# Scores, units and output projection of the first mixer in one loop: a two-layer, two-block transformer in fp32 on one core

## What is computed

```
xn = rms_norm(x, attn_norm); h = xn @ w_in          # 1024 x 2848
cq, ckv, kr, dq, dk, dv, gq, gk, gv = split(h)      # 384 256 32 512 512 512 384 128 128
q_a = rms_norm(cq) @ w_uq; k_a, v_a = rms_norm(ckv) @ w_ukv   # latent (MLA), 6 heads of 96
o_a = attention(rope(norm(q_a)), rope(norm([k_a, kr])), v_a)  # 6 maps
o_b = att(dq1, dk1, dv) - lambda * att(dq2, dk2, dv)          # differential, 4 heads, 8 maps
o_b = rms_norm(o_b) * out_gain * (1 - lambda_init)
o_c = attention(rope(norm(gq)), rope(norm(gk)), gv)           # grouped, 6 heads on 2
x = x + concat(o_a, o_b, o_c) @ w_o                 # 1280 x 1024
x = x + ffn(rms_norm(x))
```

## Time and profile before

| | |
|---|---|
| median of three runs | 2550.3 us (2546.77 to 2550.85) |
| the profiled execution | 2550.99 us, its span 2549.1 us, mean granted clock 0.944 |
| PE busy | 2344.8 us, 92% of the span |
| DVE busy | 1809.2 us, 71% |
| ACT busy | 1435.6 us, 56% |
| DMA | 570.81 MB, mean 224 GB/s |

### The profile page before, as it was taken

The page is one execution under the profiler, slowest core; times in us unless marked ns, Lnnn a source line. Parts: engine busy times, 40 slices in busy tenths (PEclk is TensorE's granted clock), DMA queues, the critical chain, the costliest instruction groups (busy, mean ns, idle before and its releaser), DMA issues. The chain is left out here.

```text
span 2549.1 us, 30005 instructions
## 1 busy us (share of the span) xinstructions
PE 2344.8 (92%) x11100; PEld 1959.6 (77%) x11100; DVE 1809.2 (71%) x2496; ACT 1435.6 (56%) x2065; POOL 76.6 (3%) x71
## 2 busy tenths in 40 slices
PE   6788999968899899889989969999999999999997
PEld 5677787757688678768877868888888888888885
DVE  4955455784555556555555657989898989898988
ACT  4433444442444444444444537878787878787876
POOL 0100000110000100000010000000000000000000
PEclk9867999986899999999999979999999999999999
DMA  6402555420455553445554337999999999999996
GB/s 238 138 1 83 190 189 183 155 93 1 143 182 188 172 181 116 133 162 186 190 185 133 113 110 262 375 334 378 337 375 339 376 338 372 341 370 338 369 347 243
DMA packets 157175, 570.81 MB, mean 224 GB/s; under 512 B 18496, under 2 KB 18816, under 8 KB 156384
## 3 DMA queue, kind: packets, MB, share of 16 engines
q1 hardware_dynamic: 153424, 553.48, 62.1%
q0 software_dynamic: 3600, 15.35, 1.8%
HBM read 567.71 MB, written 1.05 MB: 223 GB/s over the span
## 5 line engine op out<-in xcount | busy, mean ns | idle before, releaser
L368 DVE TENSOR_TENSOR w_lo<-raw,w_hi 128x1024 fp32r<-128x1024 f32 x1051 | 1270.0, 1224 | 439.7 <-ACT w_hi L362 412.0
L362 ACT CAST w_hi<-raw 128x1024 fp32r<-128x1024 f32 x1051 | 1099.0, 1052 | 472.5 <-PE bank L416 451.8
L414 PE MATMUL bank<-w_hi,x_hi 128*128 128x512 f32 (+1 forms) x2864 | 1135.0, 396 | 44.1 <-DVE x_lo L454 23.7
L416 PE MATMUL bank<-w_hi,x_lo 128*128 128x512 f32 (+1 forms) x2864 | 1114.7, 389 | 0.0
L415 PE MATMUL bank<-w_lo,x_hi 128*128 128x512 f32 (+1 forms) x2864 | 1113.0, 389 | 0.0
L414 PEld LDWEIGHTS bank<-w_hi,x_hi 128*128 128x128 f32 x2864 | 544.0, 190 | 153.8 <-issue 25.1
L416 PEld LDWEIGHTS bank<-w_hi,x_lo 128*128 128x128 f32 x2864 | 542.6, 189 | 112.9
L415 PEld LDWEIGHTS bank<-w_lo,x_hi 128*128 128x128 f32 x2864 | 544.7, 190 | 103.8
L747 PE MATMUL bank<-arena,PT 128*128 128x64 f32 (+1 forms) x576 | 96.2, 326 | 2.2 <-DVE O L764 2.2
L705 ACT ACTIVATE PP<-bank,small 128x256 f32<-128x256 f32 x80 | 37.1, 469 | 107.9 <-DVE small L695 107.9
L747 PEld LDWEIGHTS bank<-arena,PT 128*128 128x128 f32 x576 | 93.7, 247 | 2.6 <-DVE PT L734 2.4
(11 more groups left out here) (181 smaller groups left out, 1365.4 us busy)
## 6 DMA issues: line engine op xcount, KB each, us to landing
raw<-in_stream SPq DMA_DIRECT2D x1051, 512.0 KB, 5.6
tab<-in_lngb POOLq DMA_DIRECT2D x5, 1024.0 KB, 5.2
arena<-in_rpb POOLq DMA_DIRECT2D x16, 256.0 KB, 5.1
arena<-in_bgate POOLq DMA_DIRECT2D x4, 512.0 KB, 5.0
tab<-in_rowv POOLq DMA_DIRECT2D x2, 640.0 KB, 8.3
X<-in_x SPq DMA_DIRECT2D x1, 1024.0 KB, 5.2
out_y<-X SPq DMA_DIRECT2D x2, 512.0 KB, 2.8
tab<-in_ropec POOLq DMA_DIRECT2D x2, 448.0 KB, 5.1
```

Of the source, the lines that this page charges most:

```text
L362: nc.scalar.copy(w_hi[:, s % SPLIT, :], raw[:, slot, :]).then_inc(hi_done, 1)
L368: e.tensor_tensor(w_lo[:, s % SPLIT, :], raw[:, s % RAW, :], w_hi[:, s % SPLIT, :].bitcast(F32), ALU.subtract).then_inc(lo_done, 1)
L414: pe.matmul(out, xh, wh, start=first, stop=False)
L416: return pe.matmul(out, xl, wh, start=False, stop=last)
```

## The change

Four things; they act in `first_layer`, and `attention` and `unit` serve the second mixer too:

1. `w_in` is cut at the borders of its parts, seven chunks instead of six (two more halves per layer, the same columns), and the stream is reordered: cq, ckv+kr, dq, dk, then `w_uq`, `w_ukv`, then dv, gq, gk+gv; the rows of `w_o` come in the order 3, 4, 5, 6, 0, 1, 2, 7, 8, 9. The units of cq and ckv stand inside chunk dq, the units of dk inside chunk dv.
2. `attention` takes `lag`: map m's exponentials are transposed `lag` steps after its scores. The first mixer uses 2, the second 1. The transposed maps always go to bank 2, the results to bank 3. ACT copies map m-lag before it takes the exponentials of map m. In the first mixer ACT makes all copies.
3. The loop of the first mixer now holds (`fill`) the six halves of gq and gk+gv in steps 0 to 10, the DVE work of the latent and grouped heads and the norm of the differential outputs, and eight of the ten halves of `w_o` in steps 15 to 22; and (`units`) the units of the latent heads in steps 6 to 11, of the grouped heads in 12 and 13, and of the outputs in 13, 15, 17, 19, 21. The maps come in the order differential, latent, grouped. Two halves of `w_o` follow the loop.
4. `unit` replaces `qk_stage`: one ACT and one DVE instruction for both blocks. The output gain of the differential heads is applied by the unit (`og_col`) instead of by DVE.

```diff
 def chunks_in1():
-    return [(c, min(512, W_IN1 - c)) for c in range(0, W_IN1, 512)]
+    return [(C_CQ, MQR), (C_CKV, MKVR + MROPE), (C_DQ, 2 * DH * DQ), (C_DK, 2 * DH * DQ), (C_DV, DH * DV),
+            (C_GQ, GH * GD), (C_GK, 2 * GKV * GD)]
...
+        def unit(E, bk, dst, srcs, w=P, scale=1.0, gains=None, lag=1):
...
+            if E.kind == "pe":
+
+                wait(e, qk_lo, E.qk.at(1 - lag))
+                for b, src in enumerate(srcs):
+                    for tb in range(TB):
+                        i = e.transpose(pb[:, b * S + tb * P:b * S + (tb + 1) * P], src(tb), ident[:, :])
+                i.then_inc(qk_full, 1)
...
-            for step in range(M + 2):
+            for step in range(M + lag + 1):
+                m = step - lag
+                if 0 <= m < M and E.kind == "act" and by_act(m):
+
+                    copy(m)
...
-                m = step - 1
+                m = step - lag
                 if 0 <= m < M:
                     g = E.map.at(m)
-                    tbk = bank[2 if packed else 2 + m % 2]
+                    tbk = bank[2]
                     if E.kind == "pe":
                         e.wait_ge(p_ready, g + 1)
 
-                        if packed:
-                            if m:
-                                e.wait_ge(*copied(m - 1))
-                        else:
-                            wait(e, (pt_act, pt_dve)[m % 2], g // 2)
+                        if m:
+                            e.wait_ge(*copied(m - 1))
+                        wait(e, qk_lo, E.b2)
...
-                m = step - 2
+                m = step - lag - 1
...
-                        wait(e, o_done, g + 1 - (1 if packed else 3))
+                        wait(e, o_done, g)
...
-                if aside:
-                    aside(step)
+                aside(step)
+                if units:
+                    if E.kind == "pe" and lag <= step < M + lag and units(step, True):
+
+                        e.wait_ge(*copied(step - lag))
+                    units(step)
...
+            def out_half(n):
...
+                if E.kind == "pe":
+                    e.wait_ge(qk_lo, E.qk.at())
...
+                E.half_step(use)
...
+            def fill(step):
+                if step in (0, 2, 4, 6, 7):
+                    next(gq, None)
+                if step in (8, 10, 11):
+                    if step == 8 and E.kind == "pe":
+                        e.wait_ge(qk_lo, E.qk.at())
+                    next(gkv, None)
+                if step >= 15:
+                    out_half(step - 15)
+                if step < 6:
+                    latent_heads(step)
+                    made["mla"] = E.qks.at()
+                if step in (7, 8, 9):
+                    grouped(step - 7, C_GQ, GH, F_GQ, at_g)
+                    made["gq"] = E.qks.at()
+                if step == 11:
+                    diff_norm(0)
+                    grouped(0, C_GK, GKV, F_GK, at_g + TB * GH)
+                if step == 12:
+                    diff_norm(1)
+                    made["diff"] = E.qks.at()
+                    grouped(1, C_GK, GKV, F_GK, at_g + TB * GH)
+                    grouped(2, C_GK, GKV, F_GK, at_g + TB * GH)
+                    made["gk"] = E.qks.at()
...
-            attention(E, maps, latent_heads)
...
-            tp_stage(E, O, MIX // P, 0)
-            gemm_rows(E, MIX // P, 0)
+            attention(E, maps, fill, act_copies=True, units=units, lag=2)
+            out_unit(2, 9, 1, 0)
+            for n in (8, 9):
+                out_half(n)
...
-            norm_transposes(E, colg[:, l, CG_FFN:CG_FFN + KD], 4)
+            norm_transposes(E, colg[:, l, CG_FFN:CG_FFN + KD], (2, 3))
...
-            attention(E, maps, lambda step: next(job, None), packed=True)
+            attention(E, maps, lambda step: next(job, None))
```

More of the change, by code:

```diff
@@ L118, in stream_order @@
     order = list(range(TOTAL))
+    late = sum(halves_of(w) for _, w in chunks_in1()[4:])
+    for l in range(LAYERS):
+        a = l * H_L1 + H_IN1 - late
+        b = l * H_L1 + H_IN1 + H_UQ + H_UKV
+        n = H_UQ + H_UKV
+        order[a:b] = list(range(b - n, b)) + list(range(a, b - n))
+        order[b:b + H_O] = [b + k for k in O_ORDER]
     for x in range(1, NE):
@@ L603, in turned, with pair_of @@
             return i
-        def lo_block(blk):
-            return qk_l[:, blk, :]
-        def qk_stage(E, units, scaled=(), alone=False):
+        def pair_of(blk, n=2, w=P):
+            return qk_t[0:w, blk:blk + n, :], qk_l[0:w, blk:blk + n, :]
+        def unit(E, bk, dst, srcs, w=P, scale=1.0, gains=None, lag=1):
             e = E.e
[L613 to L637, removed]
@@ L639, in attention @@
-        def attention(E, maps, aside=None, packed=False):
+            hi, lo = dst
+            nb = len(srcs)
+            pb = bank[bk][0:w, 0:nb * S]
+            p3 = pb.rearrange("p (b n) -> p b n", n=S)
+            if E.kind == "pe":
[4 more added lines that the diff above has]
+                i.then_inc(qk_full, 1)
@@ L642, in attention, with by_act, copy @@
+            E.qk.n += 1
+            if bk == 2:
+                E.b2 = E.qk.at()
+        def attention(E, maps, aside, act_copies=False, units=None, lag=1):
             e = E.e
             M = len(maps)
+            O_BANK = bank[3]
+            def by_act(m):
+                return act_copies or m % 2 == 0
             def copied(m):
+                n = sum(by_act(j) == by_act(m) for j in range(m + 1))
+                return (pt_act, E.pa.at(n)) if by_act(m) else (pt_dve, E.pd.at(n))
+            def copy(m):
@@ L724, in attention @@
                         i.then_inc(pt_full, 1)
[L726 to L734, removed]
-                m = step - 2
+                    if E.kind == "dve" and not by_act(m):
+                        copy(m)
+                m = step - lag - 1
                 if 0 <= m < M:
@@ L765, in attention @@
                         i.then_inc(o_done, 1)
-                if aside:
-                    aside(step)
+                aside(step)
[3 more added lines that the diff above has]
+                    units(step)
+            E.pa.n += sum(by_act(m) for m in range(M))
+            E.pd.n += sum(not by_act(m) for m in range(M))
             E.map.n += M
@@ L819, in first_layer, with columns, four @@
             at_l = at_g + TB * ng
-            def columns(c, w):
-                return H[:, :, c:c + w]
-            def beside(chunk, hx):
-                if hx == 0 and E.kind == "dve" and chunk > 1:
+            nq, nk = MQR // P, MKVR // P
+            gg = GH // GKV
+            b_gq, b_cq = 2 * nd // 2, 2 * nd // 2 + gg + 1
+            def columns(c, n):
+                return H[:, :, c:c + n]
+            def four(c, h, d):
+                return columns(c, h * d).rearrange("p t (h d) -> p t h d", h=h)
@@ new lines, in out_half, with use @@
+            def out_half(n):
+                def use(wh, wl):
+                    k = O_ORDER[n]
+                    for tb in range(TB):
+                        t = slice(tb * P, (tb + 1) * P)
+                        for c in range(2):
+                            w = slice(c * 512, (c + 1) * 512)
+                            i = mm3(e, bank[4 + 2 * tb + c][:, :], x_hi[:, k, t], x_lo[:, k, t], wh[:, w], wl[:, w],
+                                    n == 0, n == H_O - 1)
+                    return i
+                if E.kind == "pe":
+                    e.wait_ge(qk_lo, E.qk.at())
+                    if n == 0:
+                        e.wait_ge(acc_act, E.acc.at())
+                        e.wait_ge(acc_dve, E.acc.at())
+                E.half_step(use)
```

394 lines of the change are left out of this document (266 added, 128 removed).

## The result

The changed kernel takes **2505.5 us** (median of 4 runs, 2504.5 to 2506.8) against 2550.6 for the kernel before beside it; the ratio is 0.9827, 95% interval 0.981 to 0.9844. The prediction was 2506, in a range of 2470 to 2540. Disturbed executions at a far lower clock are left out of all medians (of the run with overlapped units one in six, at 3465.9 us, which was the profiled one).

The account below looks back on a forecast made before the run. PE, 92% busy, was taken to bound the kernel through its own time and idle stretches. Mixers -45.8, norm +2.4 and second mixer -0.8 sum to -44.2 on 2550.99, giving 2506 us, range 2470 to 2540.

Parts of the forecast that it names:

- Scores of layer 0 at 95: Before the first mixer's loop: the first scores begin at 95 us instead of 117.9, 23 us earlier.
- Steps 0 to 5, 27.6: Start of the first mixer's loop: DVE sets the pace; its work and its waits for ACT take 27.6 us.
- rival (a): Better overlap: DVE's waits for ACT vanish and the clock costs 2 instead of 10 us per layer; 2475 us, chance 0.20.
- Steps 6 to 14, 45.2: Middle of the first mixer's loop: DVE sets the pace; its work and waits take 45.2 us.
- the clock's 10: First mixer's loop: low PE clock adds 10 us per layer, between 2 (always full) and 25 (low from step 6 to 17).
- Rival (c): First mixer's loop, steps 0 to 14: engines take turns without overlap, 41.5 us more per layer; 2589 us, chance 0.07.
- Steps 15 to the residual, 48.0: End of the first mixer's loop and after: PE sets the pace, 48.0 us up to the residual of `w_o`.
- Clock, low around steps 9 to 15: First mixer's loop: as a sign of being right, clock near 0.5 only around steps 9 to 15.
- Rival (b): First mixer's loop: the low clock lasts from step 6 to 17, 15 us more per layer; 2536 us, chance 0.13.
- Mixers -45.8: First mixers: the residual comes 22.9 us earlier per layer, 45.8 us in both layers.
- Norm +2.4: Ahead of the FFN: norm transposes in two banks instead of four cost 1.2 us per layer, 2.4 in all.
- The second mixer: ACT's copy now stands ahead of the exponentials ... 0: Second mixers: moving ACT's copy ahead of the exponentials, which wait for the maximum anyway, costs nothing where PE is full.

Follow-up runs that it names:

- the run without halves: Changed kernel with all ten halves of `w_o` behind the first mixer's loop instead of eight inside it; 2530.2 us, ratio 0.9928.
- copies last there: Changed kernel with ACT's copies of transposed maps behind the exponentials in the two second mixers alone; 2511.5 us, ratio 0.9845.
- the profile with four banks: Changed kernel with the four pairs of transposes ahead of the FFN in banks 2, 3, 4 and 6 instead of 2 and 3; 2502.9 us.
- the same four banks and two more edits: Changed kernel with four banks ahead of the FFN, ACT's rounding ahead of the exponentials, and step 13's units overlapped; 2480.1 us, ratio 0.9719.

## Why the prediction was right, step by step

- **Scores of layer 0 at 95**: 97.93, 2.9 late. Of this 1.6 is a slip in the sum: the terms written for `w_uq`, `w_ukv` and dv make 10.4 + 7.5 + 2.7 + 4 = 24.6, not 23.
- **Steps 0 to 5, 27.6**: 28.3 (maximum of map 0 at 98.9, of map 6 at 127.2). The terms as written make 27.2, since 25.9 - 14.4 is 11.5 and not 11.7. The waits for `w_hi` are the ones named: 2.02 where I took 2.1, 0.5 to 0.8 where I took 0.85.
- **That these waits lie on the path** (rival (a) would have been their disappearance, 7.7 per layer; "ACT's order is fixed, exponentials before rounding"): shown by turning that order round, 7.4 and 6.4 per layer.
- **Steps 6 to 14, 45.2 and most of the clock's 10**: 50.8, 5.6 over the term. Step 13 takes 8.9 of it; its stall was in the sum (3.8) and overlapping the units took 2.9 out of the step. Rival (c), the engines taking turns, is true of this step; its strongest sign in the trace, 4.0 us at map 1, cost nothing.
- **Steps 15 to the residual, 48.0**: 49.5, of which step 15 takes 8.4, more than half of it at half clock, and the next three 5.3 to 5.5, inside the 5.1 to 5.8.
- **Clock, low around steps 9 to 15**: 0.51 from 159 to 183, steps 12 to 15, and three shorter stretches before. From the first scores to the residual it is 129.6, against 130.8. The three stretches above exceed their terms by 7.8 together; that the clock's 10 is this is a difference, not a measurement. Rival (b) is out, since the clock is back at 1.00 from 183, still in step 15, but the run without halves shows how near it was: 0.50 to 208.
- **No stretch without DMA**: wrong. There is one, 159 to 183, where no half is placed.
- **Mixers -45.8**: -43.3. **Norm +2.4**: +2.6, and 1.2 per layer is what the two banks cost wherever the clock is alike.
- **"The second mixer: ACT's copy now stands ahead of the exponentials ... 0"**: this step failed. The order is worth 6 us there, mostly through the clock, which I had not looked at. The sign that I had named for it, a loop over 85 us, could not have shown it: from first to last exponentials it is 78.5 us before, 77.4 and 76.2 after, and 77.4 and 77.4 with copies last there, so that only 1.2 of the 6 us lie in the loop. In the first mixer I had given the order no price at all, and it is worth another 8.5. That the total came out to 1 us is luck in this part: my mixers were 2.5 us too good and the second mixers' 3.1 too poor.
- **Sum -44.2**: -44.8 between the spans (2549.1 to 2504.3).

## What to carry to other kernels

Where one engine works behind another, ask of each instruction which later one it stands in front of: an old map's copy behind a new map's exponentials, or a weight rounding behind them, makes a ready instruction wait for the slowest engine's current step, and turning the two round cost nothing and gave 16 us (6 of them in the second mixers, mostly the clock's) and 13.5 us here. The longest wait in a waits view need not be worth anything; look at whether the engine named there was late itself. And look for work to place in a stretch at half clock: in steps 9 to 14 here, 9 us of useless wide products per layer cost nothing, because the clock gave them back.

## What was not expected of the hardware

The second mixers, whose full steps take 5.1 us before, after and with copies last alike, come out at three lengths: over the 26 of thirteen profiles 211.0 to 211.2, 213.2 to 213.4, and 214.7 to 215.4 us. They differ in how many stretches at half clock fall near the loop's start and just behind it. In the profile with four banks they stand at 214.7 and 213.4 instead of 213.4 and 211.2, with the mixer's own code unchanged; with the same four banks and two more edits they are back at 213.4 and 211.2. There is one profile for each kernel, so it is not shown whether the edit or the execution moved them, and executions of one kernel differ too: the four banks' run from 2496.7 to 2505.4 us, those of the kernel before from 2542.4 to 2555.9. A difference of 2 to 4 us between two kernels of this sort may be no more than that. So an edit should be judged by its own stage, and that stage against another at the same granted clock, as with the FFNs above.
